# Left-over tokens on quarters of the array, an opening in halves, and a changed end

## The reference

```python
h = concatenate([meta_tokens, x])                 # 272 x 1024
proj = rms_norm(h, gain) @ w_in                   # q, k, v of two attentions, forget gates, output gates
o_a = forgetting_attention(q_a, k_a, v_a, cumsum(log_sigmoid(f_a + b)))
o_b = stick_breaking_attention(q_b, k_b, v_b)
mixed = (sigmoid(g_a) * (o_a @ w_o_fox) + sigmoid(g_b) * (o_b @ w_o_sb)) @ w_out
h = h + rms_norm(mixed);  u = conv3(rms_norm(h) @ w_up)
h = h + rms_norm((gelu(u_gate) * u_val) @ w_down);  x = h[16:]
# second block: differential attention, retention, gates, MLP, one more gated input, a last rms_norm
```

## Time and profile before

| | before |
|---|---|
| median of 3 runs | 910.97 us (910.88 to 911.46) |
| the profiled execution | 911.43 us |
| its span, first to last instruction | 910.2 us |
| mean granted TensorE clock | 0.998 |
| PE busy | 901.4 us (99%) |
| DVE busy | 681.8 us (75%) |
| ACT busy | 479.0 us (53%) |
| POOL busy | 59.4 us (7%) |

### The profile page before, as it was taken

How to read it: one execution, slowest core, us unless ns; L and a number is a source line. 1 busy time by engine, 2 the same in 40 slices (tenths; PEclk the granted TensorE clock), 3 DMA queues, 4 the chain that set the end, 5 groups by cost and what they waited for, 6 DMA issues and landing times.

```text
span 910.2 us, 17845 instructions
## 1 busy us (share of the span) xinstructions
PE 901.4 (99%) x7210; PEld 870.5 (96%) x7210; DVE 681.8 (75%) x1206; ACT 479.0 (53%) x844; POOL 59.4 (7%) x123
## 2 busy tenths in 40 slices
PE   9999999999999999999999999999999999999997
PEld 7899989999999999998999989999999999999997
DVE  8775676779888878889799877786768666666676
ACT  5366354555655445466465744554335544444456
POOL 6023000120000000000000000000102000000001
PEclk9999999999999999999999999999999999999999
DMA  8553443546556656555644363655646666666651
GB/s 320 179 159 117 139 133 119 178 139 180 158 178 203 183 169 203 181 174 179 194 149 124 116 205 119 185 185 173 187 152 185 206 188 186 185 186 185 186 156 53
DMA packets 42689, 154.72 MB, mean 170 GB/s; under 512 B 4720, under 2 KB 5232, under 8 KB 42480
## 3 DMA queue, kind: packets, MB, share of 16 engines
q1 hardware_dynamic: 42608, 153.59, 54.6%
HBM read 152.52 MB, written 1.05 MB: 169 GB/s over the span
## 4 chain that ended last, share of the span: by engine, by line
PE 97%; DVE 1%; DMA 1%; ACT 0%; SPq 0%; issue 0%
PE bank L272 96%; DMA raw<-in_wts 1%; DVE wl L1326 0%; PE bank L825 0%; PE bank L452 0%; DVE va L1955 0%; PE bank L663 0%; PE bank L664 0%; PE bank L456 0%; PE bank L455 0%; PE bank L665 0%; PE bank L454 0%; PE bank L453 0%; DVE qk L1664 0%; SPq L2026 0%
## 5 line engine op out<-in xcount | busy, mean ns | idle before, releaser
L1326 DVE TENSOR_TENSOR wl<-raw,wh 128x1024 fp32r<-128x1024 f32 x284 | 351.4, 1246 | 94.7 <-ACT wh L868 92.8
L868 ACT ACTIVATE wh<-raw 128x1024 fp32r<-128x1024 f32 x248 | 259.5, 1054 | 159.2 <-PE bank L272 148.9
L272 PE MATMUL bank<-a2h,wh 128*128 128x256 f32 x896 | 253.8, 284 | 0.1
L272 PE MATMUL bank<-a2h,wl 128*128 128x256 f32 x896 | 250.5, 280 | 0.0
L272 PE MATMUL bank<-a2l,wh 128*128 128x256 f32 x896 | 248.5, 280 | 0.0
L272 PE MATMUL bank<-a1h,wh 128*128 128x258 f32 (+1 forms) x800 | 226.1, 284 | 0.7 <-issue 0.6
L272 PE MATMUL bank<-a1h,wl 128*128 128x258 f32 (+1 forms) x800 | 223.7, 281 | 0.0
L272 PE MATMUL bank<-a1l,wh 128*128 128x258 f32 (+1 forms) x800 | 220.2, 282 | 0.0
L272 PEld LDWEIGHTS bank<-a2h,wh 128*128 128x128 f32 x896 | 168.8, 188 | 3.2 <-issue 2.9
L272 PEld LDWEIGHTS bank<-a2h,wl 128*128 128x128 f32 x896 | 168.6, 188 | 0.0
L272 PEld LDWEIGHTS bank<-a2l,wh 128*128 128x128 f32 x896 | 167.6, 188 | 0.3
(11 more groups left out here) (245 smaller groups left out, 1007.9 us busy)
## 6 DMA issues: line engine op xcount, KB each, us to landing
raw<-in_wts SPq DMA_DIRECT2D x284, 512.0 KB, 3.8
csb<-in_cst SPq DMA_DIRECT2D x1, 1428.0 KB, 10.0
out<-va SPq DMA_DIRECT2D x2, 512.0 KB, 3.0
xc<-in_xT SPq DMA_DIRECT2D x1, 544.0 KB, 5.5
raw<-in_wts SPq DMA_DIRECT2D x2, 256.0 KB, 3.3
xc<-in_xT SPq DMA_DIRECT2D x1, 276.0 KB, 3.0
xc<-in_xT SPq DMA_DIRECT2D x1, 272.0 KB, 4.3
va<-in_pT SPq DMA_DIRECT2D x1, 256.0 KB, 3.9
```

Source lines behind the costliest of these rows:

```text
L272: return e.matmul(o, lhsT, rhs, start=start, stop=stop, skip_group_check=True)
L868: e.activation(wh[:, i % NHL, :], raw[:, i % NRAW, :], ACT.Copy).then_inc(s_hi, 1)
L1326: e.tensor_tensor(lo, src, hi.bitcast(F32), ALU.subtract).then_inc(s_lo, 1)
```

## The change

It has three parts. (1) The left-over tokens are multiplied in plain float32, straight from `raw`, four slices k at a time, each on its own 32 columns of the array (output rows 32j to 32j + 31 of one bank); DVE adds the four groups of rows, and the way out of VA's banks is split between ACT and DVE. Because TensorE now reads `raw`, the loads of blocks 4 to 11 also wait for `s_blk`. (2) Blocks 1 and 2 are split in halves, as block 0 was. (3) At the end the turning of tiles 4 to 7 moves behind the sums.

```diff
 def values(...):
-                    if i0 + q:
+                    if i0 + q > 2:
                         e.wait_ge(s_lo, i0 + q + 1)
...
-                        if meta is not None:
-                            e.wait_ge(s_meta, 4 * k + 2 + (2 if m0 == 0 else 0))
-                            mm(bank[meta][:, :], a1h[:, k, m0:m0 + 128], mh, k == 0, False)
-                            t = mm(bank[meta][:, :], a1h[:, k, m0:m0 + 128], ml, False, k == KT - 1)
+                        if meta is not None and kk and q % 2:
+                            e.wait_ge(s_meta, 2 * k + (1 if m0 else 2))
+                            for j in range(4):
+                                t = mm(bank[meta][32 * j:32 * j + 32, :], tokf[:, k - 3 + j, m0:m0 + 32],
+                                       raw[:, (i0 + q - 1 + j // 2) % NRAW, j % 2 * 512:j % 2 * 512 + 512], q == 1, q == 3)
                         if kk:
                             t.then_inc(s_blk, 1)
 # SyncE
             def load(i):
                 if i >= NRAW:
                     e.wait_ge(s_lo, i - NRAW + 1)
+                if NRAW <= i < B_F + NRAW:
+                    e.wait_ge(s_blk, (i - NRAW) // 2 * 2 + 2)
 # VectorE
+            def meta_out(n, d, o, r_meta, copied):
+                if not copied:
+                    e.wait_ge(s_pad, 3)
+                    e.tensor_copy(d, o[0:NM, :]).then_inc(s_vp, 1)
+                for j in range(1, 4):
+                    e.wait_ge(s_vp, n + j)
+                    e.tensor_tensor(d, o[32 * j:32 * j + NM, :], d, ALU.add).then_inc(s_vp, 1)
+                e.wait_ge(s_vp, n + 4)
+                e.tensor_scalar(d, d, r_meta[0:NM, :], None, ALU.mult).then_inc(s_vm, 1)
...
-            values_out(B_VA, 4, lambda c: va[:, 3 + c, :], 3, (4, 5), r_tok0[:, 2:4], r_tok0[:, 5:6])
...
+                if t == 1:
+                    meta_out(4, va[0:NM, 3, :], bank[3], r_tok0[:, 5:6], True)
 # ScalarE, after the high part of block 11
+                    e.activation(va[0:NM, 3, :], bank[3][0:NM, :], ACT.Copy).then_inc(s_vp, 1)
+                    for c in range(2):
+                        e.activation(va[:, 4 + c, :], bank[4 + c][:, :], ACT.Identity,
+                                     scale=r_tok0[:, 2 + c:3 + c]).then_inc(s_va, 1)
 # GpSimd: 16 scalings of 128x16 numbers in place of 32 copies
+                for n, t0 in enumerate((S, 0)):
+                    e.tensor_scalar(tokf[:, k, 32 - 32 * n:32 - 32 * n + NM], hT[:, k, t0:t0 + NM], g0[:, k:k + 1], None,
+                                    ALU.mult).then_inc(s_meta, 1)
 # TensorE, the end
-            for n in range(3, 6):
-                turn_out(n)
+            turn_out(3)
...
-                if m == 6:
-                    turn_out(6)
+                if m == 7:
+                    turn_out(4)
...
-            turn_out(7)
+            for n in range(5, 8):
+                turn_out(n)
```

More of the change, by code:

```diff
@@ L192, in program @@
         s_rtc0 = sem("s_rtc0")
+        s_vp = sem("s_vp")
         s_va, s_evA, s_evD = sem("s_va"), sem("s_evA"), sem("s_evD")
@@ L232, in ev2 @@
             return (s_evA if c == "A" else s_evD), EV1.count(c) + EV2[:t + 1].count(c)
+        tokf = va[:, 6, :].rearrange("p (k c) -> p k c", k=KT)
         FD = lambda m: bank[4 + m // 2][:, (m % 2) * S:(m % 2) * S + S]
@@ L325, in values @@
                         k = 2 * q + kk
-                        if i0 + q == 0:
-                            e.wait_ge(s_lo if kk else s_l0, 1)
+                        if i0 + q <= 2:
+                            if kk:
+                                e.wait_ge(s_lo, i0 + q + 1)
+                            else:
+                                e.wait_ge((s_l0, s_l1, s_l2)[i0 + q], 1)
                         mh, ml = wh[:, s, kk * 512:kk * 512 + 512], wl[:, s, kk * 512:kk * 512 + 512]
@@ L362, in sb_scores @@
                 if pair == 0:
-                    e.wait_ge(s_va, 8)
+                    e.wait_ge(s_va, 4)
                     e.wait_ge(s_vm, 2)
@@ L504, in tensor_engine @@
                 if t == 0:
+                    e.wait_ge(s_vp, 4)
+                elif t == 1:
+                    e.wait_ge(s_va, 1)
+                elif t == 2:
                     e.wait_ge(s_va, 2)
[L506 to L509, removed]
                 elif t == 3:
@@ L645, in diff_scores @@
                 if h == 0:
-                    e.wait_ge(s_va, 10)
+                    e.wait_ge(s_va, 6)
                 else:
@@ L672, in diff_av @@
                 if h < 2:
-                    e.wait_ge(s_va, 12)
+                    e.wait_ge(s_va, 8)
                 else:
@@ L890, in scalar_engine @@
                 input_hi(k)
+                if k == 5:
+                    e.wait_ge(s_raw[2], 16)
+                    e.activation(wh[:, 2, 0:512], raw[:, 2, 0:512], ACT.Copy).then_inc(s_h2, 1)
+                    e.activation(wh[:, 2, 512:1024], raw[:, 2, 512:1024], ACT.Copy).then_inc(s_hi, 1)
+                    made["n"] = 3
                 if k % 2:
@@ L1396, in vector_engine @@
             e.wait_ge(s_rtc0, 6)
-            values_out(B_VB, 0, lambda c: va[:, (2, 0, 1)[c], :], 0, (1, 2), r_tok0[:, 0:2], r_tok0[:, 4:5])
+            e.wait_ge(s_blk, B_VB + 4)
+            meta_out(0, va[0:NM, 2, :], bank[0], r_tok0[:, 4:5], False)
+            for c in range(2):
+                e.tensor_scalar(va[:, c, :], bank[1 + c][:, :], r_tok0[:, c:c + 1], None, ALU.mult).then_inc(s_va, 1)
             for q in range(4):
                 lo_to(B_VA + q + 4)
-            values_out(B_VA, 4, lambda c: va[:, 3 + c, :], 3, (4, 5), r_tok0[:, 2:4], r_tok0[:, 5:6])
             def forget():
```

59 lines of the change are left out of this document (28 added, 31 removed).

## The result

The changed kernel takes 920.72 us (median of 4 runs, 918.74 to 923.80) against 911.12 us of the kernel before (4 runs, 910.88 to 911.46). The ratio is 1.0108, with a 95% interval from 1.0094 to 1.0122: 9.6 us slower. The profiled run was the quickest of the four, 918.74 us with a span of 917.5 us; it holds one fall of the granted TensorE clock, where a second profile of the same kernel, of a run near the median, holds two (experiments 6 and 7).

What follows compares the result with a forecast made beforehand. TensorE, busy 99% of the span with 97% of the chain, was taken as the bound. 911.43 us (profiled) + 6.5 opening - 0.2 end = 917.7, or 917.3 for the median; range 914.0 to 922.0.

Steps and rivals of the forecast that it cites:

- the rival with two falls of the clock: TensorE's clock falls in the opening's two gaps: one fall 918.7 to 919.3 us, two 921; chance 28%.
- the likeliest case of 917.3: Whole kernel: both opening gaps occur, with no clock fall, 917.3 us for the median; chance 44%.
- Bound: Whole kernel: TensorE is busy 99% of the span, so what delays it once is hardly ever caught up.
- Group of quarters, 1.15 us: Left-over tokens in VB and VA: four float32 matmuls side by side on 32 columns each take 1.15 us a group.
- The rival's 2 us for each us of a group: Quarters not four at a time: 2 us lost per us; two at a time 919.0, serial 923.7; chance 15%.
- The sum waits for the tree: VB, before the sum of squares: TensorE waits over 1 us for DVE's tree, hiding halves and first group.
- First round: Loads 6 and 7 wait for block 3, at 22.2 us: gap of 3.9 us before block 7.
- Second round: Loads 10 and 11 wait for block 7: gaps of 0.6 us before t = 2 and 3.3 before the scores.
- The rival that half closes, 914.0: Second gap, before the scores, closes because something ahead is quicker: 3.3 us less, 914.0 us; chance 6%.
- The opening together: From the start to the first scores: +6.5 us, scores at 53.95 instead of 47.47.
- The end: Last 5 us, turned tiles behind the sums: output half at 905.1 instead of 905.36, -0.2 us.
- The other side: Opening: the loads' wait costs nothing, blocks 6, 7, 10 and 11 land in time: 909.6 us; chance 7%.

Runs made afterwards that it cites:

- experiments 6 and 7: 6: changed kernel unaltered again, 920.33 us; 7: changed kernel with 13 idle float32 matmuls each ahead of block 7 and the scores, 918.11 and 917.63 us.
- experiment 11: Changed kernel with loads of blocks 4 to 7 into free memory, sum of squares one slice later, VA's additions before low part of 11: 909.52 us.
- experiment 9: Kernel before with only the high and low parts of blocks 1 and 2 made in halves: 911.50 us, ratio 0.9993.
- experiment 8: Changed kernel with all four float32 matmuls of a group on the same 32 columns of the array: 925.09 us, ratio 1.0157.
- Experiment 2: Changed kernel with the low part of block 7 ahead of the reductions and VB's way out on DVE: 915.41 us, ratio 1.0044.
- Experiment 3: Changed kernel with VA's way out earlier: ACT's share before the high part of block 10, DVE's before the low part of block 9: 916.08 us.
- experiment 1: Changed kernel with blocks 4 to 7 loaded into unused memory, so no load waits for a recent block: 910.49 us, ratio 0.9992.
- experiment 5: Kernel before with only the added wait of the loads of blocks 4 to 11 for TensorE: 917.70 us, ratio 1.0068.
- experiment 4: Changed kernel with low part of block 7 ahead of VB's way out and VA's way out moved earlier: 913.14 us, ratio 1.0019.

## Why the prediction was right

The time lay in the range and the sign was right; 920.7 us is the rival with two falls of the clock ("two: 921"), not the likeliest case of 917.3. The mechanism of the opening came out as written, gap by gap; the 3.4 us between 917.3 and the median did not come from it. Point by point:

- **Bound.** Every us lost in the opening reached the end but for the clock: 53.71 - 47.47 = 6.24 at the scores, -0.25 at the end, +1.5 for the one fall, together 7.5; the profiled runs differ by 918.74 - 911.43 = 7.3.
- **Group of quarters, 1.15 us.** From the last full matmul before a group, with the usual 0.46 us for its two, to the start of the next are 1.08 us more, and that next one takes 0.11 us longer: 1.19 us. From block 1 to block 8, with no waits in either, it is 25.06 us with four groups (experiment 11) and 26.86 with 28 low-part matmuls (experiment 9): 1.80 us less, and 28 x 0.233 - 4 x 1.19 = 1.76. Four on one quarter take 3.62 us (experiment 8), so the serial end of 3.7 was sized right and four abreast are 3.4 times as fast. The Trainium skill (TensorE: Matmul & The Clock Gate, Part 3) has 2.38 times for three column tiles. This trace has 3.4 (3.62 against 1.07 us) for four: a loss too, but a smaller one, and the group came out at 1.19 us, not at the 1.4 that I had estimated from that figure. The rival's 2 us for each us of a group was near: 2.55 us a group cost 5.59 at the scores.
- **The sum waits for the tree.** 1.17 us, sum at 19.29, VB's end at 22.34; predicted over 1 us, 19.2 and 22.2. Halves and first group were indeed hidden there: with the sum moved and the loads free, they show (experiment 11).
- **First round.** The high part of block 5 begins at 19.76 instead of 19.07, so the held loads of blocks 4 and 5 land somewhat later, not "at the same time"; it cost nothing. Load 6 out at 22.52 and landed after 3.5 us (predicted 22.2 and 4.1), high part 26.07 (26.3), low part of 6 at 27.16 (27.45), low part of 7 at 34.16 (34.4). The gap was 3.22 for 3.9, since TensorE also came 0.5 us later to block 7. Block 8: 39.42 (39.6). Experiment 2 confirms what stood ahead: VB's way out moved behind the low part of 7 takes this gap away.
- **Second round.** 0.14 us before t = 2 (0.6), 3.33 us before the scores (3.3), scores at 53.71 (53.95). Experiment 3 confirms VA's additions in that place: moved away, they take this gap with them, and cost 1.40 us before block 9 where they then stand. The rival that half closes, 914.0, needed an order that the changed kernel does not have.
- **The opening together**: +6.24 us (+6.5). **The end**: -0.25 us in the profile, -0.18 alone (-0.2).
- **What was off** is the choice among the cases: "The forecast itself has 44%", the clock's fall 28%. The sum of 917.3 us is that of a run without a fall. I priced the low clock at up to 2 us a fall; it is 1.5 in the changed kernel. 917.3 + 2 x 1.5 = 920.3 us, against 920.72 and 920.33 measured. That the usual run has both falls is argued from this sum, from one profile (920.07 us) and from the mean clocks; it is not shown for each run. In the trace of before the 1.03 us of the earlier trace rows was the longest gap of the opening and no guide to one of 3 us; what did point to it was the earlier trace rows, where the clock is down a little over 1 us after TensorE's last instruction, and I gave it too little weight.
- **The other side**, a hold that costs nothing, was priced at 909.6; with the hold made harmless (experiment 1) the scores are 0.67 us sooner and the end 0.24: 911.43 - 0.67 - 0.24 = 910.5 us for a profiled run, 910.1 for a median. The profile of experiment 1 took 911.46 us, 1.0 more, all of it in a later stretch (last section), and its median 910.49, with a ratio of 0.9992. So my 1.2 us for the opening was 0.67; 0.40 of the difference is the wait before the scores that is left.

## What to carry to other kernels

When a second engine begins to read a staging buffer, the buffer's refill waits for the slower reader: look at what the refill's late data must still pass on the engines between it and the consumer, for the list there can cost as much as the transfer. Look up the order of each list in the kernel that is timed: experiment 5 was mispredicted by using another kernel's, and experiment 3 put its work one block too early. Price a gap of several us in TensorE's work with the clock that may fall behind it, 1.5 us a time here and 2.9 once, and put long evacuations behind the preparation that TensorE wants next.

## What the runs showed of the hardware that I had not expected

- **The clock does not fall each time.** Gaps with a fall at their end or shortly behind: 3.33 (first profile), 3.20 and 3.35 (second), 3.10 (experiment 8), and 2.38 (experiment 2, where 2.9 us were lost). Gaps without: 3.22 (first profile), 3.34 (experiment 3), 2.37 (experiment 5). In the opening, gaps up to 1.40 us never had one. What decides between the equal ones stays open. At the end of experiment 11's profile the clock is low from 901.96 on, in the last six transposes and with no wait of TensorE just before; from the first matmul on the last gate tiles (895.45) its end took 12.05 us instead of 11.8. In experiment 2's profile the same six transposes took 1.27 us instead of 0.85 and its end 12.24 us. So the changed end, which puts these six behind the sums, lost its 0.2 us in two of eleven profiles; why there is open. The other runs of experiment 5 have mean clocks of 0.995 to 0.997 and 917.1 to 919.1 us, against 0.998 and 915.35 of the profiled one, so its median probably has falls too; that is argued from the mean clock alone.
- **A stretch with two lengths.** From the first `bank<-a2h,wh` to the first `bank<-wh,a2h` (214.46 to 414.16 before) it takes 199.5 to 199.7 us in ten profiles, and 200.7 us in those of experiments 1 and 4 and in both of 7, at full clock and with no gap more. The two kernels that were profiled twice showed the same length both times, so it may hang on the kernel; the runs do not settle it. It adds 1.0 us to those four and explains why experiment 4 met its 913.2 us with scores 1.3 us sooner than expected. From there to the first matmul on the last gate tiles (414.16 to 898.16 before) it is 483.9 to 484.1 us in eleven profiles, 483.2 in those of experiments 5 and 8, and 484.7 in that of experiment 3, which is 0.7 us of its miss. Where kernels are compared to 1 us, the place in the trace is surer than the total.
